# Two-layer transformer block on one core: gate units released by silu, and the modulation rows of the first FFN placed in other down stages

## The reference, cut to what matters

```python
def swiglu(h, wg, wu, wd):
    return (jax.nn.silu(h @ wg) * (h @ wu)) @ wd

c_act = jax.nn.silu(c)
for i in range(DEPTH):
    mod = c_act @ ada_w[i] + ada_b[i]
    sh1, sc1, g1, sh2, sc2, g2, sh3, sc3, g3 = jnp.split(mod, N_MOD, axis=-1)
    h = modulate(rms_norm(x, ln_ffn1[i]), sh1, sc1)
    x = x + 0.5 * g1[:, None, :] * swiglu(h, ffn1_wg[i], ffn1_wu[i], ffn1_wd[i])
    ...
```

## Time and profile before

| what | us |
|---|---|
| median of three executions (2556.73 to 2558.82) | 2558.21 |
| the profiled execution, its own time | 2556.32 |
| its span, from the first to the last instruction | 2554.5 |
| TensorE (PE) busy in the span | 2503.3 (98%) |
| VectorE (DVE) busy | 1457.9 (57%) |
| ScalarE (ACT) busy | 1109.0 (43%) |
| GpSimd (POOL) busy | 1109.0 (43%) |

### The profile page before, as it was taken

The page is one execution under the profiler, slowest core; times in us unless marked ns, Lnnn a source line. Parts: engine busy times, 40 slices in busy tenths (PEclk is TensorE's granted clock), DMA queues, the critical chain, the costliest instruction groups (busy, mean ns, idle before and its releaser), DMA issues.

```text
span 2554.5 us, 36310 instructions
## 1 busy us (share of the span) xinstructions
PE 2503.3 (98%) x14578; PEld 2182.6 (85%) x14578; DVE 1457.9 (57%) x2045; ACT 1109.0 (43%) x1933; POOL 1109.0 (43%) x578
## 2 busy tenths in 40 slices
PE   6999998999999999999999999999999999999999
PEld 5787887776878989889999988999988888889998
DVE  6757476445576635767545257454566555564543
ACT  3222224555523635524544434444554444534544
POOL 2445443322355655446564434565640000455553
PEclk8999999999999999999999999999999999999999
DMA  8676664211273333442333322324322221223322
GB/s 297 227 241 231 214 214 157 80 53 67 78 245 109 113 99 100 165 165 83 116 98 100 101 83 83 116 89 139 95 87 86 73 73 50 83 95 111 108 84 83
DMA packets 249244, 312.52 MB, mean 122 GB/s; under 512 B 7356, under 2 KB 227149, under 8 KB 248950
## 3 DMA queue, kind: packets, MB, share of 16 engines
q1 hardware_dynamic: 246762, 308.88, 36.6%
q10 hardware_dynamic: 2316, 1.33, 0.2%
HBM read 308.07 MB, written 4.74 MB: 122 GB/s over the span
## 4 chain that ended last, share of the span: by engine, by line
PE 89%; DVE 5%; issue 1%; DMA 1%; ACT 1%; POOL 1%; SPq 0%; DVEq 0%; ACTq 0%
PE bank L2321 12%; PE bank L2322 11%; PE bank L2326 11%; PE bank L2378 8%; PE bank L2381 8%; PE bank L2379 8%; PE bank L2338 6%; PE bank L2339 5%; PE bank L2343 5%; PE bank L2304 1%; PE bank L2306 1%; PE bank L2305 1%; PE bank L2393 1%; PE bank L2394 1%; PE bank L2395 1%
## 5 line engine op out<-in xcount | busy, mean ns | idle before, releaser
L938 POOL TENSOR_TENSOR w_lo_t<-w_raw,w_hi_t 128x1024 fp32r<-128x1024 f32 (+1 forms) x284 | 710.0, 2517 | 1179.3 <-ACT w_hi_t L1111 1178.8
L1111 ACT CAST w_hi_t<-w_raw 128x1024 fp32r<-128x1024 f32 (+1 forms) x316 | 311.1, 1026 | 379.8 <-PE bank L2326 204.5
L932 POOL TENSOR_TENSOR w_lo_t<-w_raw,w_hi_t 128x512 fp32r<-128x512 f32 x232 | 323.4, 1409 | 240.8 <-ACT w_hi_t L1124 238.5
L2321 PE MATMUL bank<-h_hi,w_hi_t 128*128 128x512 f32 x720 | 282.0, 392 | 6.1 <-DVE bank L1990 6.0
L2321 PE MATMUL bank<-act_hi,w_hi_t 128*128 128x512 f32 x720 | 282.3, 392 | 5.8 <-ACT w_hi_t L1111 5.4
L2322 PE MATMUL bank<-act_lo,w_hi_t 128*128 128x512 f32 x720 | 281.6, 391 | 0.0
L2322 PE MATMUL bank<-h_lo,w_hi_t 128*128 128x512 f32 x720 | 280.3, 389 | 0.0
L1682 DVE SCALAR_TENSOR_TENSOR scr<-scr,cact 128x1024 f32<-128x1024 f32 x112 | 208.0, 1857 | 61.6 <-DMA scr<-in_ada_w 54.4
L2378 PE MATMUL bank<-t_hi_t,w_hi_t 128*128 128x256 f32 x928 | 232.8, 283 | 0.0
L2379 PE MATMUL bank<-t_lo_t,w_hi_t 128*128 128x256 f32 x928 | 232.7, 283 | 0.0
L2026 DVE SCALAR_TENSOR_TENSOR x<-bank,half,x 128x512 f32<-128x512 f32 x88 | 65.9, 749 | 243.9 <-PE bank L2326 174.1
(11 more groups left out here) (316 smaller groups left out, 5722.4 us busy)
## 6 DMA issues: line engine op xcount, KB each, us to landing
scr<-in_ada_w SPq DMA_DIRECT2D x128, 512.0 KB, 5.4
w_raw<-in_ffn_wg SPq DMA_DIRECT2D x44, 1024.0 KB, 5.4
w_raw<-in_ffn_wu SPq DMA_DIRECT2D x44, 1024.0 KB, 5.3
w_raw<-in_ffn_wd SPq DMA_DIRECT2D x32, 1024.0 KB, 5.3
w_raw<-in_mlp_w SPq DMA_DIRECT2D x32, 1024.0 KB, 5.3
w_raw<-in_hgrn_w_in SPq DMA_DIRECT2D x16, 1024.0 KB, 5.4
w_raw<-in_ffn_wd SPq DMA_DIRECT2D x16, 768.0 KB, 4.6
w_raw<-in_attn_w_qkv SPq DMA_DIRECT2D x12, 1024.0 KB, 5.1
```

Source lines behind the costliest of these rows:

```text
L932: nc.gpsimd.tensor_tensor(piece(w_lo_q, t, j), raw_quarter(t, n, k), piece(w_hi_q, t, j).bitcast(F32), ALU.subtract).then_inc(w_lo, 1)
L938: nc.gpsimd.tensor_tensor(w_rows(w_lo_t, t, k.start, k.stop), w_raw[:, t % 2, k], w_rows(w_hi_t, t, k.start, k.stop).bitcast(F32), ALU.sub ...
L1111: act.copy(w_rows(w_hi_t, t, k.start, k.stop), w_raw[:, slot, k]).then_inc(w_hi, 1)
L2321: pe.matmul(dst, w, blk(m_hi, kb), start=kb == 0, stop=False)
```

## The change

It has three parts. (1) A gate unit of a pair other than the first waits for `act1`, the silu that read its bank one pair ago, and no longer for `v_done`, VectorE's product of that pair. (2) In the first FFN of layer 0 the steps of the down stages go from 8, 8, 8 to 12, 12, 0; the sum stays 24. Behind the units nb = 0 to 3 stand two steps each and behind nb = 4 to 7 one each; before it was one behind each of the 8 in down 0 and down 1, and two behind each of nb = 0 to 3 in down 2. (3) SyncE issues tile 0 and tile 1 of such a stage with no row between them, then the rows of nb 0 and 1, tile 2, the rows of nb 2 and 3, tile 3, and the rows of nb 4 to 7.

```diff
 def down_steps(op, nb):
 
-    per = 2 if op.last else 1
-    return range(op.c0 + min(op.ada, per * nb), op.c0 + min(op.ada, per * nb + per))
+    return range(op.c0 + min(2 * nb, 4 + nb), op.c0 + min(2 * nb + 2, 5 + nb))
...
-    def ffn(layer, which, gate, ada, std=(8, 8, 6), down_ada=0):
+    def ffn(layer, which, gate, ada, std=(8, 8, 6), down_ada=(0, 0, 0)):
...
-                          ada=down_ada))
+                          ada=down_ada[g]))
...
-            ffn(layer, "ffn1", 0, (24, 24, 16), down_ada=8)
+            ffn(layer, "ffn1", 0, (24, 24, 16), down_ada=(12, 12, 0))
...
                             if op.ada:
-                                for nb in (4 * i + 2 * s, 4 * i + 2 * s + 1):
+                                for nb in ((), (0, 1), (2, 3), (4, 5, 6, 7))[2 * i + s]:
                                     for step in down_steps(op, nb):
                                         ada_step(step)
...
                             for b in range(2):
-                                if s == 0:
+                                if s == 0 and i:
+                                    pe.wait_ge(act1, 2 * i + (op.v0 + b - 1))
+                                elif s == 0:
                                     pe.wait_ge(v_done, 2 * i + (op.v0 + b + 1))
```

## The result

The changed kernel takes 2543.5 us (four executions, 2543.1 to 2543.7); the kernel before took 2557.5 us with one more execution beside it (2556.7 to 2558.8). The ratio is 0.9946, 95% interval 0.9930 to 0.9961: 14.1 us less, faster by more than the 0.2% bound. The forecast was 2543.2.

What follows compares the result with a forecast made beforehand. TensorE, busy for 98% of the span, was taken as the bound. Savings of 6.9 us at gate units and 8.1 us in down 2, 15.0 in sum, took 2558.2 to 2543.2 us; range 2540.5 to 2550.5.

Steps and rivals of the forecast that it cites:

- Gate units wait for silu: Gate units of pairs other than the first: five stalls go whole, 6.2 us, a sixth shrinks 0.7; 6.9 us saved.
- cover of 10.9 us: Up unit of the next pair: needs VectorE's late product only 10.9 us after the gate unit, against 1.7 us lateness.
- No rows in down 2: Down 2: without steps and row loads, tile 2 goes out earlier and its 8.1 us stall goes whole.
- the fourth row had to wait for a step: Down 2 before the change: the fourth row waited for a VectorE step behind unit 1; tiles 2 and 3 followed it.
- Four more rows in down 0 and down 1: Down 0 and down 1: more rows and steps cost 0; bounds 0 and 8.1 us for tile 3 in down 0.
- third rival: Down 0: tile 3 lands late or GpSimd's low part does; up to 8.1 us lost, likelier 2; chance 0.11.
- cover of 1.2 to 4 us: Down 0, tile 3: lands at 164.5 to 167.3 and may land at 168.5, so no cost.
- An addition may be 5.44 - 0.7 us late before a unit waits: VectorE in down 0 and down 1: groups of 3.3 to 6.0 us against 5.44 per unit, so cost 0.
- a step's price, 2.65 us: VectorE's modulation steps: 1.27 us each alone, 2.65 where GpSimd works beside them, taken as the most.
- First (tile 3 of down 2): Down 2: tile 3's low part or an addition comes up to 3.5 us late, time 2546.7; chance 0.14.
- Second (release moves to the up units): Up units, or another name, still wait for VectorE's product; the gate saving yields nothing, time 2550.1; chance 0.06.
- Fourth: Down 0, down 1 and next up stages: four-row bursts hold weights, 4 x 8.1 = 32.4 us lost, 2575.6; chance 0.03.

Runs made afterwards that it cites:

- the third chip: The changed kernel again, unedited, beside the kernel before on another chip: 2543.10 us, ratio 0.9942.

## Why the prediction was right, point by point

**The time** was met within 0.3 us, the saving less well: 15.0 forecast, 14.1 by medians. The kernel before came out 0.7 us lower with one more execution, which hid part of a missed cost of 1.4 us; that the time was met so closely is partly luck. On the third chip the saving was 15.2 with that cost still in the trace, so only the matched traces show it.

**Gate units wait for silu.** Forecast 6.9, measured (matched) 7.2 alone and 7.1 in the full change. The 7.3 by the medians of the part alone holds the 1.15 lost in down 2 as well, so it is no measure of the gate units alone. The seventh place, 0.3 us at 1093, is too short to stand among the waits; it shows only as a late start. The shorter wait at 1574.92 gave the 0.7 us expected and was ended by ScalarE, as said. The cover of 10.9 us at the up units held everywhere. The restart cost beside the idle time, about 0.3 us for each wait, was needed to get the sum.

**No rows in down 2.** Forecast 8.1, measured 8.1, and tile 3 was not late. That the low clock went with the idle stretch was worth about 2.4 of them, worked out in the last section. The clock had fallen within the stretch, not after it; that changed no term, since the 8.06 was read from the groups' starts. The order of transfers in down 2 alone takes the stall away and leaves 3.0 us to VectorE, so the step "the fourth row had to wait for a step" was the cause, as read.

**Four more rows in down 0 and down 1.** The queue's part was right: tile 3's cast in down 0 was forecast at 163 to 167 and came at 165.47, with 1.7 us of cover for the cast and 0.9 for the low part. The third rival stayed away by the smaller of them, and the prediction's cover of 1.2 to 4 us counted only the cast. VectorE's part failed. The step was: "An addition may be 5.44 - 0.7 us late before a unit waits; from nb = 4 on each group is half as long. Cost 0." I had set one group of at most 6.0 us against one unit of 5.44, but tile 0's two units are worked block by block together and end 1.4 us apart (at about 276.3 and 277.6), so two groups and a transpose stand ahead of unit 2's addition. And the upper end of a step's price, 2.65 us, was a mean over up-stage steps of which part ran with GpSimd; beside GpSimd throughout it was 6.09 / 2 = 3.05. Cost 1.4 us, and the experiments with other spreads take it away.

**The parts as a sum.** I added terms as if each stood alone. They don't: the rows alone cost 1.7 us at gate units of up 1 by the shift of the transposes, and the gate part alone makes down 2's stall 1.15 us longer. In the full change both vanish, so the sum came out right, but each part's own worth did not follow from it.

**The rivals.** First (tile 3 of down 2): 4.15 us of low parts from 396.2 on were done at 400.4, in time; not seen in the changed kernel, but its near relative, a unit held 3.0 us by a late addition, is what the order alone met. Second (release moves to the up units): excluded by the gate part alone. Third: a stall in down 0 did not come; the stall came in down 1, on VectorE. Fourth: undoing the order shows its mechanism, at tile 2 of down 0 and of down 1, for 8.7 and 7.6 us, so its price of 8.1 each was fair. The rule of the Trainium skill (SBUF — State Buffer, section Who interferes with whom), that a VectorE instruction with two SBUF inputs contends with a GpSimd instruction that reads SBUF, spoke to the right place: the slowed steps are what made the new wait, though through VectorE's additions and not through GpSimd's low parts as I had it. That GpSimd's work is the cause of the slow steps rests on their overlap and on the run with the order undone, where the same two steps took 2.67 us with GpSimd idle; no run moved GpSimd's work alone, and the step that GpSimd's start fell into at 278.79 was not slowed.

## What to carry to other kernels

In a queue that holds both weights and optional rows, ask of each row what its issue waits for: a row that waits for work of the stage itself makes the weights behind it as late as that work. Let a writer of a bank wait for the reader of that bank, not for the end of the chain behind it; no up unit paid for it here, and it hides delays that later changes bring in. And when background steps are dealt out behind units, count by the times at which units end, not by unit: two that end 1.4 us apart share one slot.

## What the runs showed of the hardware

An idle stretch of TensorE costs more than its length, and the surplus jumps. Waits of 1.36 us cost 1.69, and one of 2.7 us (the order of down 2 alone) cost 3.0, both with no low clock: a surplus of 0.2 to 0.3. The four longer waits all have a stretch at a granted clock of 0.50, the 1.2 GHz level, that begins within the wait:

| wait | us idle | us cost | surplus | at 0.50, us | of these after the wait |
|---|---|---|---|---|---|
| order undone, down 1 | 4.6 | 7.6 | 3.0 | 6.8 | 5.9 |
| before, down 2 | 5.4 | 8.1 | 2.7 | 6.8 | 5.2 |
| gate part alone, down 2 | 6.2 | 9.2 | 3.0 | 10.2 | 6.0 |
| order undone, down 0 | 6.8 | 8.7 | 1.9 | 6.8 | 3.5 |

The surplus follows the last column and not the idle time. In the low stretch matmuls of 512 columns start 0.427 us apart, at full clock 0.227, so 1 - 0.227 / 0.427 = 0.47 of that time is lost; with the 0.3 of the short waits this gives 3.1, 2.7, 3.1 and 1.9. A longer wait can so cost a smaller surplus, when more of the low stretch passes while TensorE is idle anyway, and two kernels that differ only in where a stall lies can differ by more than the stall.

Short waits can have a low stretch too: with the steps spread otherwise, waits of 1.0 and 1.8 us in up 1 were followed by 3.4 us at 0.50, where the single wait of 2.7 us was not. One kernel's profiles also differed by a stretch of 3.4 us at that level in the attention, 0.8 to 0.9 us, with the same idle time ahead of it. What decides in these cases is open.
